# Column-ordered inputs, a first layer interleaved with its projections, and router logits made by rows

## What is computed

```python
# first layer (l = 0); x: [256, 1024], mem: [256, 1024]
mkv = mem @ w_mem_kv[l]                      # keys and values of the memory, two layers
h = x @ a_w_in[0]                            # q k (4 heads x 96), v r (4 x 192), g (16), m (4 x 64)
log_a = log_sigmoid(g @ a_w_gate2 + a_b_gate) / 16
o = gla(q, k, v, log_a)                      # gated linear attention, chunks of 64, state carried on
o = o * rsqrt(mean(o * o) + 1e-6) * a_norm_g # per head
mix = silu(r) * o
mo = softmax(m @ km.T / 8) @ vm              # attention over the memory, 4 heads
x = layer_norm(alpha * x + concat(mix, mo) @ w_out[0])
# then a product-key expert layer, a dilated-attention layer, another such expert layer,
# and two layers with attention and a mixture of experts whose router is
logits = x @ w_router + b                    # [256, 4 groups + 16 experts]
group = argmax(logits[:, :4])                # then the 2 best of the group's 4 experts, softmax weights
```

## Time and profile before

| | |
|---|---|
| time, median of 3 runs | 2860.3 us (2859.81 to 2861.45) |
| the profiled execution | 2862.17 us, its span 2860.2 us |
| granted TensorE clock, mean | 0.982 |
| TensorE busy | 2742.7 us, 96% |
| VectorE, ScalarE, GpSimd busy | 70%, 47%, 11% |
| moved | 479 MB, 167 GB/s |

### The profile page before, as it was taken

One profiled execution on the slowest core, in us unless ns is written; L12 is line 12 of the kernel. 1 busy time (PEld: TensorE's weight loads), 2 busy tenths in 40 slices (PEclk: granted clock), 3 DMA queues, 4 the chain that ended last, 5 costly groups with the idle time before them and its releaser, 6 DMA issues.

```text
span 2860.2 us, 43908 instructions
## 1 busy us (share of the span) xinstructions
PE 2742.7 (96%) x17298; PEld 2407.5 (84%) x17298; DVE 2001.6 (70%) x3889; ACT 1345.8 (47%) x2188; POOL 302.5 (11%) x162
## 2 busy tenths in 40 slices
PE   7999999999999999999999999999999899898997
PEld 7779999998888888799999988888777678786776
DVE  4676988985555655679889755556657759656588
ACT  3423554444445534435454444455235357453465
POOL 0003950000000001049400000000110000000000
PEclk9999999999999999999999999999999999999999
DMA  5344554555665644445544555656421359532586
GB/s 191 113 136 126 177 175 157 155 164 184 195 194 191 223 147 133 142 133 177 170 157 157 167 185 195 194 192 210 125 89 24 125 193 355 185 99 68 174 296 226
DMA packets 175116, 479.04 MB, mean 167 GB/s; under 512 B 27184, under 2 KB 43456, under 8 KB 174912
## 3 DMA queue, kind: packets, MB, share of 16 engines
q1 hardware_dynamic: 171808, 473.29, 50.5%
q10 hardware_dynamic: 3104, 2.95, 0.3%
HBM read 474.61 MB, written 1.57 MB: 166 GB/s over the span
## 4 chain that ended last, share of the span: by engine, by line
PE 87%; DVE 7%; ACT 3%; POOL 2%; issue 1%; DMA 0%; SPq 0%; DVEq 0%; ACTq 0%; POOLq 0%
PE ps L134 86%; POOL ring_rest L154 2%; PE ps L137 2%; DVE spl L154 1%; DVE big L162 1%; ACT big L140 1%; DVE st L178 1%; ACT whi L140 1%; DVE big L154 1%; DVE xb L162 1%; DVE st L162 0%; ACT spl L140 0%; DVE xr L154 0%; POOL big L154 0%; DVE grouped L154 0%
## 5 line engine op out<-in xcount | busy, mean ns | idle before, releaser
L140 ACT ACTIVATE whi<-ring 128x1024 fp32r<-128x1024 f32 x512 | 542.5, 1060 | 686.6 <-PE ps L134 684.7
L134 PE MATMUL ps<-xr,whi 128*128 128x256 f32 x4096 | 750.4, 285 | 11.1 <-POOL ring_rest L154 10.7
L154 DVE TENSOR_TENSOR ring_rest<-ring,whi 128x1024 fp32r<-128x1024 f32 x412 | 503.5, 1222 | 318.1 <-ACT whi L140 318.1
L134 PEld LDWEIGHTS ps<-xr,whi 128*128 128x128 f32 x4096 | 640.4, 193 | 14.0 <-DVE big L184 8.6
L134 PE MATMUL ps<-whi,Ar 128*128 128x512 f32 x2048 | 631.1, 389 | 4.5 <-DVE Ar L154 4.5
L134 PE MATMUL ps<-xr,ring_rest 128*128 128x256 f32 x2048 | 580.8, 284 | 0.0
L154 DVE TENSOR_TENSOR spl<-ring,spl 128x1024 fp32r<-128x1024 f32 (+3 forms) x384 | 435.3, 1163 | 124.9 <-ACT spl L140 115.8
L134 PEld LDWEIGHTS ps<-whi,Ar 128*128 128x128 f32 x2048 | 384.5, 188 | 84.4 <-DVE Ar L154 4.9
L140 ACT ACTIVATE spl<-ring 128x1024 fp32r<-128x1024 f32 (+3 forms) x384 | 373.4, 1008 | 94.5 <-PE ps L134 75.6
L134 PE MATMUL ps<-ring_rest,Ar 128*128 128x512 f32 x1024 | 398.4, 389 | 0.0
L134 PEld LDWEIGHTS ps<-xr,ring_rest 128*128 128x128 f32 x2048 | 394.4, 193 | 0.0
(11 more groups left out here) (127 smaller groups left out, 2488.6 us busy)
## 6 DMA issues: line engine op xcount, KB each, us to landing
ring<-in_peer_u_dram SPq DMA_DIRECT2D x256, 512.0 KB, 3.5
ring<-in_peer_v_dram SPq DMA_DIRECT2D x256, 512.0 KB, 3.5
ring<-in_moe_gate_up_dram SPq DMA_DIRECT2D x128, 512.0 KB, 5.0
ring<-in_moe_w_down_dram SPq DMA_DIRECT2D x64, 512.0 KB, 5.1
ring<-in_peer_w_q_dram SPq DMA_DIRECT2D x32, 512.0 KB, 4.6
ring<-in_sb_w_in_dram SPq DMA_DIRECT2D x24, 512.0 KB, 4.8
ring<-in_ab_w_in_dram SPq DMA_DIRECT2D x20, 512.0 KB, 6.0
ring<-in_w_out_dram SPq DMA_DIRECT2D x16, 512.0 KB, 4.7
```

Of the source, the lines that this page charges most:

```text
L134: return self.e.matmul(o, l, r, start=start, stop=stop)
L140: return self.e.activation(o, i, f, **k)
L154: return self.e.tensor_tensor(o, a, b, op)
```

## The change

- Copies of x and mem with features first (`x_turned`, `mem_turned`) are made on the host, as other inputs are, and loaded in two halves each; ScalarE and VectorE split them out of SBUF (`split_quarter`). x is loaded by rows as well, for the norm. TensorE's 32 transposes go. x's first two quarters are split beside the last step of `mkv1`. ScalarE issues the small loads after mem's quarters.
- `Ag` is the first projection. The banks are fixed: `Ag` 4 to 6, `Aq` and `Ak` 0 to 3, `Av` and `Ar` 0 and 1, `Aw` and `As` 2 and 3.
- The steps of the memory attention run beside the projections (`A_AT`), without fillers; scores in banks 4 and 5, turns in 6, outputs in 7. `heads_pe` and its two companions are split in functions of one step, otherwise as they were. Chunk products, states and the rows of tile 0 are hooks of steps 10 to 12.
- ScalarE squares the rows out of PSUM with a running sum; one inverse root serves both tiles; the product reads PSUM. The silu is in two parts. `rows_pe`, `states_pe`, `states_dve`, `chunks_pe`, `chunks_dve` hold what stood in `gla_pe` and `gla_dve`, with fixed banks, and no stage ends in a `join`.
- Router: x is stationary and the weights move, so that logits come as 128 x 20 per tile; ScalarE's copy and the two transposes go, 9 fillers become 10. `first` has one step less, the places five. The rests of `xrow` move: tile 0 behind the group's one-hot, tile 1 behind `P01`.

The diff, cut to its core ("e" is an engine, "P" TensorE, "A" ScalarE, "V" VectorE):

```diff
+        def beside_plan(jobs):
+            plan = {}
+            for s in range(len(jobs)):
+                plan["scores", s] = 4 if total(jobs[s]) > 512 else 4 + s % 2
+                plan["turn", s], plan["out", s] = 6, 7
+            return plan
...
+        def turned_load(sp, name, dst):
+            for h in range(2):
+                c = slice(4 * h, 4 * h + 4)
+                sp.dma_start(dst[:, c, :], io[name + "_turned"][:, c, :]).then_inc(arrival(f"{name}{h}"), 16)
...
+            turned_load(sp, "mem", memT)
+            load_unit(sp, ("mkv0", 0))
...
+            turned_load(sp, "x", xT)
...
+        def split_quarter(e, name, key, src, q):
+            c = slice(2 * q, 2 * q + 2)
+            if e.name == "A":
+                e.wait_ge(arrival(f"{name}{q // 2}"), 16)
+                e.activation(xr[:, 0, c, :], src[:, c, :], ACT.Copy).then_inc(*acted.next((key, q)))
+            else:
+                e.wait_ge(*acted.at((key, q)))
+                e.tensor_tensor(xr[:, 1, c, :], src[:, c, :], xr[:, 0, c, :].bitcast(F32), ALU.subtract).then_inc(
+                    *vec.next((key, q)))
...
+        def start_beside(e):
+            def beside(i, k):
+                if i == 3 and k == 2 and e.name in "AV":
+                    for q in range(2):
+                        if e.name == "A":
+                            e.wait_ge(*psum.at((("mkv1", 0), "used", 1)))
+                        split_quarter(e, "x", "x0", xT, q)
+            return beside
+        def start_end(e):
+            for q in range(2, 4):
+                if e.name == "A":
+                    e.wait_ge(*psum.at(("mkv1", 3)))
+                split_quarter(e, "x", "x0", xT, q)
         def start_act(act):
+            for q in range(2):
+                split_quarter(act, "mem", "mem", memT, q)
+            round_unit(act, ("mkv0", 0))
+            for q in range(2, 4):
+                split_quarter(act, "mem", "mem", memT, q)
             for name, dst, src in SMALL:
                 act.dma_start(dst, src, allow_slow_non_contiguous=True).then_inc(arrival(name), 16)
...
+            project_all(act, mkv, "mem", 1, None, start_beside(act))
+            start_end(act)
             need(act, stored(mkv, *[(1, n) for n in range(4)]))
             act.dma_start(kept, kvm[1]).then_inc(arrival("kept"), 16)
...
         def start_pe(pe):
+            project_all(pe, mkv, "mem")
             pe.wait_ge(arrival("cst"), 16)
...
-        projA = [projection("Aq", WA, 0, 384, [Tcols(96 * h, 96, qA[:, h, :]) for h in range(4)]),
+        projA = [projection("Ag", WA, 2304, 272, [Tcols(0, 128, gT, 16), Tcols(16, 128, qmT[:, 0, :]),
+                                                  Tcols(144, 128, qmT[:, 1, :])]),
+                 projection("Aq", WA, 0, 384, [Tcols(96 * h, 96, qA[:, h, :]) for h in range(4)]),
                  projection("Ak", WA, 384, 384, [Tcols(96 * h, 96, kA[:, h, :]) for h in range(4)]),
...
                  projection("Av", WA, 768, 512, Nrows(0, 512, lambda t: vA[:, t, 0:512])),
                  projection("Aw", WA, 1280, 256, Nrows(0, 256, lambda t: vA[:, t, 512:768])),
...
+        for p_, b_ in zip(projA, (4, 0, 0, 0, 2, 0, 2)):
+            p_["base"] = b_
...
-        HOOKS_A = {"V": {2: [tables_dve], 6: [gate_dve], 8: [log_dve], 9: [scan_dve], 11: [qk_dve], 13: [kend_dve]},
-                   "A": {2: [tables_act], 7: [abs_act], 8: [log_act], 10: [exp_act], 12: [end_act]},
-                   "P": {6: [gate_pe]}, "G": {12: [end_pool]}, "S": {}}
...
+        def squares_act(act, t):
+            for h in range(4):
+                act.wait_ge(*psum.at(("gla", t, h // 2)))
+                act.activation(mix[:, t, 192 * h:192 * h + 192], bank(gla_bank(t, h // 2))[:, 192 * (h % 2):192 * (h % 2) + 192], ACT.Square,
+                               accum_out=ss[:, 4 * t + h:4 * t + h + 1]).then_inc(*acted.next(("squares", t)))
...
+        def silu_act(act, k):
+            need(act, stored(projA, (5 + k, 0), (5 + k, 1)))
+            d = slice(512 * k, 512 + 256 * k)
+            act.activation(rA[:, :, d], rA[:, :, d], ACT.Silu).then_inc(*acted.next(("silu", k)))
...
+        A_AT = [(3, 0), (3, 2), (4, 0), (4, 2), (5, 0), (5, 2), (6, 0), (6, 2), (7, 0), (7, 2), (8, 0), (8, 2), (9, 0), (9, 2)]
+        def gla_beside(e):
+            def beside(i, k):
+                if (i, k) in A_AT:
+                    heads_step(e, "memA", jobsA, planA, buffersA, A_AT.index((i, k)))
+            return beside
+        HOOKS_A = {"V": {0: [tables_dve], 2: [gate_dve, log_dve], 4: [scan_dve], 6: [qk_dve], 8: [kend_dve], 10: [chunks_dve],
+                         11: [lambda e: states_dve(e, 0), lambda e: states_dve(e, 1)], 12: [lambda e: states_dve(e, 2)]},
+                   "A": {1: [tables_act], 2: [abs_act], 3: [log_act], 5: [exp_act], 7: [end_act], 12: [lambda e: silu_act(e, 0)]},
+                   "P": {2: [gate_pe], 10: [chunks_pe], 11: [lambda e: states_pe(e, 0), lambda e: states_pe(e, 1)],
+                         12: [lambda e: states_pe(e, 2), lambda e: rows_pe(e, 0)]},
+                   "S": {11: [lambda e: load(e, "norm_g", lambda r: [(r[:, 0:768], io["a_norm_g"].to_broadcast([128, 768]))],
+                                             (vec, ("r", 1)))]}}
...
+        def gla_finish(e, name, following):
+            def turn_rows(k):
+                marks = [(vec, ("mixA", t, k)) for t in range(2)]
+                out_turn(e, name, k, marks if k else [(vec, ("memA", "stored", 7))], (3, 6, 4, 7)[k])
+            if e.name == "P":
+                rows_pe(e, 1)
+            elif e.name == "A":
+                squares_act(e, 0)
+                silu_act(e, 1)
+                round_unit(e, (name, 0))
+                squares_act(e, 1)
+            elif e.name == "V":
+                gains_dve(e, 0)
+                rest_unit(e, (name, 0))
+                gains_dve(e, 1)
+            if e.name in "PAV":
+                turn_rows(0)
+                out_both(e, name, 0, following)
+            if e.name == "V":
+                for t in range(2):
+                    e.wait_ge(*acted.at(("squares", t)))
+                step(e, e.tensor_scalar(ss, ss, 1.0 / 192.0, HEAD_EPS, ALU.mult, ALU.add))
+                rsqrt(e, rn, ss, wk)
                 for h in range(4):
                     d = slice(192 * h, 192 * h + 192)
+                    for t in range(2):
+                        o = bank(gla_bank(t, h // 2))[:, 192 * (h % 2):192 * (h % 2) + 192]
+                        e.stt(mix[:, t, d], o, rn[:, 4 * t + h:4 * t + h + 1], rA[:, t, d], ALU.mult, ALU.mult).then_inc(
+                            *vec.next(("mixA", t, h)))
             if e.name == "P":
...
+                busy(e, 6)
             if e.name in "PAV":
...
                 for k in range(1, 4):
...
+                    turn_rows(k)
                 for k in range(1, 4):
                     out_both(e, name, k, following)
...
         def moe_pe(pe, l, xk):
             w = halves(("rt", l))
-            take(pe, 0)
+            take(pe, 0, 2)
             for c in range(8):
                 pe.wait_ge(*vec.at((xk, c // 2)))
                 pe.wait_ge(*lo.at((("rt", l), c // 4)))
-                ins = mm3(pe, ps[0:20, 0, 0:T], [a[:, c % 4, :] for a in w[c // 4]], xs(c), c == 0, c == 7)
+                for t in both_t:
+                    ins = mm3(pe, ps[:, t, 0:20], xs(c, t), [a[:, c % 4, :] for a in w[c // 4]], c == 0, c == 7)
                 between_pe(pe, xk, c)
             ins.then_inc(*psum.next(*spent(("rt", l)), ("logits", l)))
...
+                give(pe, t, (vec, ("rows", l)))
+            busy(pe, 10)
             take(pe, 2)
...
-            act.wait_ge(*psum.at(("logits", l)))
-            act.activation(lgT, ps[0:20, 0, 0:T], ACT.Copy).then_inc(*acted.next(("logits", l)))
...
             def first(o, v, top):
                 step(dve, dve.tensor_tensor(eq, v, wide(top), ALU.is_equal))
-                step(dve, dve.tensor_scalar(eq, eq, -100.0, 100.0, ALU.mult, ALU.add))
-                step(dve, dve.tensor_tensor(eq, eq, it4, ALU.add))
+                step(dve, dve.tensor_tensor(eq, eq, it4, ALU.mult))
                 step(dve, dve.reduce(idx, eq, ALU.min))
                 return dve.tensor_tensor(o, it4, wide(idx), ALU.is_equal)
...
+            def xrow_rest(t):
                 dve.wait_ge(*hi.at(("xrow", l, t)))
                 dve.tensor_tensor(xrow[:, t, 1, :], xb[:, t, :], xrow[:, t, 0, :].bitcast(F32), ALU.subtract).then_inc(
                     *lo.next(("xrow", l, t)))
+            row4 = C("iota", 128, 0, 4)
+            it4 = under.unsqueeze(1).to_broadcast([128, 2, 4])
+            step(dve, dve.tensor_scalar(under, row4, -100.0, None, ALU.add))
+            step(dve, dve.tensor_scalar(starts, row4, 128.0, 256.0, ALU.mult, ALU.add))
             for name in (f"mbg{l}", f"mbr{l}"):
                 dve.wait_ge(arrival(name), 16)
-            dve.wait_ge(*psum.at(("rows", l)))
```

(15 more changed lines are left out.)

481 lines of the change are left out of this document (214 added, 267 removed).

## The result

The changed kernel takes 2847.6 us (median of 5, 2847.1 to 2848.9). Runs of the kernel before beside it took 2861.45 (2859.8 to 2862.2): ratio 0.9942, 95% interval 0.9931 to 0.9954. The forecast was 2840 with a range of 2833 to 2850, faster; the direction and the range held, but about 5 of the forecast 20 us are missing, between the profiled executions as between the medians 6. The profiled execution took 2847.1 us, its span 2845.3, 14.9 under the span of before.

What follows compares the result with a forecast made beforehand. TensorE, 87% of the last-ending chain, was taken as the bound, with time going only to its waits and filler. Start and first layer -19.0 and routers -1.2 gave 2842.0, or 2840 as median; range 2833 to 2850.

Steps and rivals of the forecast that it cites:

- rival (b): First layer: VectorE's hooks delay head steps, another 0.7 us in each of 14, +10, 2850 (2846 to 2856); chance 0.22.
- The first step: Start: first weight half lands at about 7, so TensorE starts at about 9.4, 7.5 us earlier.
- The second step: Start: small DMAs behind mem's fourth quarter take ScalarE's queue 6.1 us, delaying roundings to 18.7; TensorE stalls 1.2 and some 0.4.
- The keys' wait: First layer: query and key projections share banks 0 to 3, so keys wait for the last copy, +1.0 us.
- The 5 us allowed for head steps: First layer: fourteen head steps among the projections, each a switch with waits in program order, 0.35 each, +5 us.
- only shift: Everything between 190 and 2220 us is untouched and should only move, some 19 us earlier.
- the price of a pair: Routers: a pair of column groups by rows, 12 matmuls of 20 columns, costs 1.25 us (0 to 1.44) instead of 0.72.
- all turns slide by 1.7: First router: at low clock twelve matmuls cost 2.4 us, sliding all turns by 1.7; net 0.3 us faster taken there.
- (a): Whole kernel: the overlap works as priced, 2840 us (2834 to 2845); chance 0.60.
- (c): First layer: better, allowance of 5 us not needed and clock high in the tail, 2834 or less; chance 0.11.
- (d): First layer: slower than before, head steps standing over 1.4 us more each at banks 6 and 7; 2868 at 2 us; chance 0.04.
- (e): Routers: fillers, the late rest of tile 1 and low clock take the gain back; 2842.5, counted within (a)'s range.

Runs made afterwards that it cites:

- logits_by_columns: The changed kernel with only the router's logits undone (by columns, copy, two transposes, nine fillers); shorter index steps and moved rests stay: 2840.9 us, ratio 0.9928.
- first_layer_only: The changed kernel with the whole router of the kernel before: 2844.4 us, ratio 0.9939.

## Why the prediction was right, and where it wasn't

The time lies in the range, and the first layer did what was forecast of it. Two things in that are luck. At k = 1 the forecast is 0.1 off because its errors cancel: the start came out 1.6 better, the projections 1.4 worse. And the whole stays under 2850 only because the range had been left wide for rival (b), while the loss came from the routers, 8.6 us beside their forecast.

**Start.** Forecast: TensorE at 9.4, a stall of 1.6 behind the small issues, layer A at 40.75. Measured 10.62, no stall, 39.16. The first step was too early because the weights landed at 8.16, not at 7. The second step failed as a mechanism: the issues didn't wait for ScalarE's copies ahead of them, as the sum had it (10.3 + 6.1), but ran beside them from 9.51 and took 5.4. The rounding behind them did stand 3.32, as forecast in kind, but began at 14.93; its rest was made by about 17.3 and TensorE, which came to it at 17.90, didn't wait. Moving the issues in front cost 1.7.

**Projections and what went among them.** Forecast 90.55 from the first projection to the last (40.75 to 131.3), measured 91.9. The keys' wait was forecast at 1.0 and is 1.01. The 5 us allowed for head steps was the right size for the wrong reason: all waits but the keys' make 0.84. The mean clock of 0.97 is 5.5 us at half, which cost 2.8 where 1.7 was forecast. The remaining 3.5 us or so are busy time beyond the sum; which matmuls are slower than priced isn't shown.

**Tail.** Forecast 17.1 from the last projection to k = 1, measured 17.2. The squares needed no table load; k = 0 begins 6.4 behind the end instead of 8.1, because the squares of tile 0 began before it and those of tile 1 at E+3.3 instead of E+4.2. The clock in the tail (131.1 to 148.3) stays at 1.00, so the 0.7 charged for it isn't paid; the idle before k = 0 is 1.69, not 3.6. Together -19.8 at k = 1, where the prediction's own time, 148.4, is 0.1 off.

**Untouched stages "only shift".** Not quite. Between k = 1 and router 1 the kernel gained another 1.6, in stages where code is equal. Two such stages in windows, before and after:

```profile
194.00:198.00 4.00, 4.00 (x28) 3.84 (x27) 3.49 (x9) 0.60 (x1) 0.00 (x0) 0.77 0.00 0
...
253.00:257.00 4.00, 0.96 (x4) 0.99 (x5) 4.00 (x28) 2.35 (x3) 3.46 (x2) 0.61 0.38 131
```

```profile
174.00:178.00 4.00, 4.00 (x33) 3.76 (x33) 3.72 (x9) 0.60 (x1) 0.00 (x0) 1.00 0.02 4
...
232.00:236.00 4.00, 0.69 (x5) 0.72 (x6) 4.00 (x28) 2.61 (x3) 3.20 (x2) 0.97 0.41 131
```

Low stretches of 3 to 10 us come out longer, shorter or not at all when the work lies elsewhere in time. The three stretches of equal code in the table of marks came out at -1.6, +0.55 and -1.45, and the time at half clock in them went from 41 to 34, from 17.1 to 20.5 and from 24.7 to 22.2: the same signs. Between the two routers, where the code is equal in all these kernels, the length follows the time at half clock: 342.4 us with 17.1 (before), 343.0 with 20.5 (after), 346.7 with 27.3 (logits_by_columns), 348.3 with 30.7 (first_layer_only), some 0.4 us for each us at half clock. What decides where a low stretch falls in one execution stays open.

**Routers.** Forecast -1.2 with bounds of -2.2 and +2; measured +7.4. The steps of VectorE came out: rank to permutation 1.10 shorter (forecast 1.1), the stand for the rest of tile 1 0.97 (forecast 1.0), the `first` calls 0.4 (forecast 0.4). The failed term is the clock under the logits and the ten fillers, not the price of a pair: that was put at 1.25 and is 1.36 from start to start (the 1.03 us for ten records behind it is the distance of weight loads; the row cited has 1.28 busy), and where the clock is full, in router 2, the ten fillers begin 15.84 us behind the norm's first filler, against 15.8 forecast. The prediction took the low clock of router 1 as given (3.4 us), whereas under the new matmuls it lasts 17.1. There the ten fillers begin at 21.84, 6.0 later than at full clock, and take 3.8 instead of the 2.1 forecast; in router 2 they take 3.9, since the clock falls under them. The four pairs of router 1 are busy for 10.7 against 4.3 before. The sentence that twelve matmuls cost 2.4 at the low clock was nearly right (2.59 from start to start); what was wrong is "all turns slide by 1.7" once, for a cost that repeats in each group, and fillers at 0.21 each.

**The rule on the clock.** The prediction cited the Trainium skill (TensorE: Matmul & The Clock Gate, What's actually happening) for the tail, that half rate is the default and activity lifts it. In the tail the runs show nothing of it, since the clock stayed at 1.00 across idle times of 1.69 and 1.71. In the routers they agree in part: the changed kernel's low stretches ended under fillers of 512 columns. But TensorE counts as busy for 17.00 of 17.00 us at 0.50 in router 1, so busy time in a profile doesn't tell by itself whether the clock comes back: with 20 columns the clock stayed low, with 120 it was back sooner. The prediction weighed the rule for idle time alone, and not for narrow work.

**Rivals.** (a) was right for the first layer, but the whole ended 2.6 above its own range. The time fits (b), whose mechanism didn't happen; nor did (c) or (d), though the clock was high in the tail as in (c). (e) named the right place, clock and fillers included, at 2.5 us where it was 8.6 (from -1.2 to +7.4).

## What to carry to other kernels

Before a wide matmul is turned round so that a few columns move and the wide side is loaded as weights, price the clock as well as the weight loads: here the 20-column matmuls of a pair cost 1.7 times the wide ones at full clock, and under them TensorE was at half clock for 17 us. A filler that seems to delay a product may be what brings the clock back, so look at which clock it and what follows it run before it is cut: six fewer in each router brought 0.9 us and not 4.6. A gain in one place can come with half-clock stretches far away in equal code, and be lost there; compare distances between marks within a trace, not only totals, when an effect is below 5 us.
